# The gate and value stages of a decoder step as straight code, with the index and coefficient tables read in place

## What is computed

```python
q = (xt @ w_query)                     # 8 heads
s1, s2 = q[..., :half] @ k1.T, q[..., half:] @ k2.T
v1, i1 = top_k(s1, 16); v2, i2 = top_k(s2, 16)
top, pos = top_k(v1[:, None] + v2[None, :], 16)
eidx = take(i1 * 128 + i2, pos)        # 8 x 16 = 128 experts a token
g = softmax(top)
hid = einsum("thkd,td->thk", u_tab[eidx], xt)
out = einsum("thk,thkd->td", g * gelu(hid), v_tab[eidx])
```

## Time and profile before

| what | us |
|---|---|
| median of three runs | 1786.53 (1786.04 to 1788.68) |
| the profiled execution | 1785.46 |
| its span, first to last instruction | 1783.8 |
| TensorE busy | 1679.1 |
| VectorE busy | 1403.2 |
| ScalarE busy | 765.6 |
| GpSimd busy | 581.5 |

### The profile page before, as it was taken

One profiled execution on the slowest core, in us unless ns is written; L12 is line 12 of the kernel. 1 busy time (PEld: TensorE's weight loads), 2 busy tenths in 40 slices (PEclk: granted clock), 3 DMA queues, 4 the chain that ended last, 5 costly groups with the idle time before them and its releaser, 6 DMA issues.

```text
span 1783.8 us, 30227 instructions
## 1 busy us (share of the span) xinstructions
PE 1679.1 (94%) x9914; PEld 1487.4 (83%) x9914; DVE 1403.2 (79%) x3186; ACT 765.6 (43%) x1194; POOL 581.5 (33%) x513
## 2 busy tenths in 40 slices
PE   5999998788999999989989999997999999999997
PEld 4999743468999999979989999996888888888885
DVE  3225368446399899969989999997899999999998
ACT  3223145123344432346767777763333333333333
POOL 0000370000445443653333324334333333333331
PEclk9999999799899999999999999998999999999999
DMA  3344451550433332479998999999999999999995
GB/s 117 98 161 149 148 181 42 196 224 1 141 111 131 118 108 96 164 256 357 386 355 311 395 343 382 415 391 371 377 382 386 387 384 383 389 385 383 385 388 184
DMA packets 195266, 470.85 MB, mean 264 GB/s; under 512 B 17971, under 2 KB 100531, under 8 KB 192607
## 3 DMA queue, kind: packets, MB, share of 16 engines
q1 hardware_dynamic: 134430, 254.46, 40.7%
q0 software_dynamic: 50944, 178.96, 26.6%
q10 hardware_dynamic: 9792, 36.18, 5.1%
HBM read 411.97 MB, written 61.32 MB: 265 GB/s over the span
## 4 chain that ended last, share of the span: by engine, by line
PE 40%; DVE 26%; issue 6%; DMA 2%; ACT 1%; DVEq 0%; SPq 0%; ACTq 0%; POOLq 0%
PE va L232 10%; PE va L233 10%; PE va L231 10%; DVE og L1925 3%; DVE gathered L1473 3%; PE hp L231 3%; PE hp L232 3%; PE hp L233 3%; DVE ulo L1949 2%; PE ggp L1869 2%; DVE vw L1473 2%; DVE eq L1732 1%; DVE sc L1684 1%; DVE oh L1924 1%; DVE X L1691 1%
## 5 line engine op out<-in xcount | busy, mean ns | idle before, releaser
L231 PE MATMUL hp<-mid_hi,uhi 128*128 128x384 f32 x1024 | 360.3, 352 | 29.4 <-DVE ulo L1949 18.0
L232 PE MATMUL hp<-mid_lo,uhi 128*128 128x384 f32 x1024 | 349.4, 341 | 0.0
L233 PE MATMUL hp<-mid_hi,ulo 128*128 128x384 f32 x1024 | 347.9, 340 | 0.0
L232 PE MATMUL va<-vlo,ahi 128*128 128x512 f32 x768 | 298.8, 389 | 0.0
L231 PE MATMUL va<-vhi,ahi 128*128 128x512 f32 x768 | 298.8, 389 | 0.0
L233 PE MATMUL va<-vhi,alo 128*128 128x512 f32 x768 | 298.8, 389 | 0.0
L1807 POOL DMA_INDIRECT gathered<-in_v_experts,idx_row x160 | 189.7, 1185 | 331.6 <-DVEq L2252 270.3
L231 PEld LDWEIGHTS hp<-mid_hi,uhi 128*128 128x128 f32 x1024 | 196.2, 192 | 35.1 <-DVE ulo L1949 20.8
L1385 POOL TENSOR_TENSOR ulo<-uw,uhi 128x1024 fp32r<-128x1024 f32 x49 | 123.2, 2515 | 262.0 <-ACT uhi L1381 261.9
L1815 ACT ACTIVATE vhi<-vw 128x1024 fp32r<-128x1024 f32 x128 | 134.8, 1053 | 155.7 <-DMA vw<-in_v_experts 153.4
L232 PEld LDWEIGHTS hp<-mid_lo,uhi 128*128 128x128 f32 x1024 | 196.4, 192 | 0.0
(11 more groups left out here) (337 smaller groups left out, 3355.5 us busy)
## 6 DMA issues: line engine op xcount, KB each, us to landing
uw<-in_u_experts SPq DMA_DIRECT2D x128, 512.0 KB
vw<-in_v_experts SPq DMA_DIRECT2D x128, 512.0 KB
gate_matrix<-gst ACTq DMA_DIRECT2D x12, 2048.0 KB
hidden_values<-gelu_out SPq DMA_DIRECT2D x72, 192.0 KB
hd<-hidden_values SPq DMA_DIRECT2D x16, 768.0 KB
gt<-gate_matrix SPq DMA_DIRECT2D x16, 768.0 KB
uw<-hidden_values SPq DMA_DIRECT2D x16, 768.0 KB
uw<-gate_matrix SPq DMA_DIRECT2D x16, 768.0 KB
```

Source lines behind the costliest of these rows:

```text
L231: nc.tensor.matmul(out, a_hi, b_hi, start=first, stop=False)
L232: nc.tensor.matmul(out, a_hi, b_lo, start=False, stop=False)
L233: return nc.tensor.matmul(out, a_lo, b_hi, start=False, stop=last)
```

## The change

The loops of both stages are unrolled. `over_turns` and the value stage run plain Python loops, so every instruction has a constant address. With that go `idx_row`, `hrow`, `crow`, the copies into them, `keep`, and the semaphores `idx`, `hrow`, `part`, `crow`, `fetched`, `init`, `clear`. Gathers take their index column from `eidx`, dots write to `hid`, and adds read `coef`.

Waits that change: the first u gathers wait for `eidx` itself; `cut` waits for `oh` two chunks back rather than for `part`; a gather of `v` waits for the add that used its buffer (`s0` or `s1`), and in row 0 for the last dot that used it, rather than for all dots; these five are asked for in the order in which their buffers come free, behind the memset of `acc_s`. The order of `ulo`, the last dots and `vlo` on VectorE at the seam stays.

One thing more changes: VectorE's share of expert rows. No row is added with tiles 0 to 3, then 160 x (m - 3)/120 rows are done by tile m, up to tile 123, and none with the last four. VectorE also doesn't wait for the start value of `acc0` ahead of the work on tile 4.

```diff
-        def request(pool, n, pairs=0):
+        def request(pool, n):
             row, b = divmod(n, ROW)
             if n == 0:
+                pool.wait_ge(table_prep, 1)
+            if n == SG:
                 pool.wait_ge(gs["tab"], 1)
-            if n == SG:
-                pool.wait_ge(gs["idx"], LOOK)
-            if row and b == 0:
-                pool.wait_ge(gs["idx"], row + 1 + PAIR_ROWS * pairs)
             if n >= LOOK:
-                pool.wait_ge(gs["dot"], n - LOOK + 1 + PAIR_ROWS * ROW * pairs)
-            fetch(pool, n % LOOK, row % LOOK, b)
+                pool.wait_ge(gs["dot"], n - LOOK + 1)
+            fetch(pool, n % LOOK, row, b)
...
-                dve.wait_ge(table_prep, 2)
-                nc.vector.tensor_copy(idx_row[:, :, 0:SG], eidx[:, 0:LOOK, 0:SG]).then_inc(gs["tab"], 1)
                 dve.wait_ge(table_spread, 16 * SG)
-                nc.vector.tensor_copy(eidx[:, 0:SR, SG:], spread_idx[:]).then_inc(gs["tab"], 1)
-                dve.wait_ge(gs["tab"], 2)
-                nc.vector.tensor_copy(idx_row[:, :, SG:], eidx[:, 0:LOOK, SG:]).then_inc(gs["idx"], LOOK)
+                nc.vector.tensor_copy(eidx[:, :, SG:], spread_idx[:]).then_inc(gs["tab"], 1)
...
-        def fetch_v_row(pool, r, slot, b):
-            if b == 0:
-                pool.wait_ge(xs["idx"], r + 1)
-            pool.wait_ge(xs["fetched"], r * ROW + b + 1)
+        def fetch_v_row(pool, r, b):
+            if r == 0:
+                pool.wait_ge(gs["dot"], users(b, LAST_DOTS)[-1] + 1)
+            elif b < SG:
+                pool.wait_ge(xs["s0"], (r - 1) * SG + b + 2)
+            else:
+                pool.wait_ge(xs["s1"], r + 1)
...
         def over_turns(eng, turn):
-            with eng.Fori(0, NI // 2 - 1) as pair:
-                turn(pair, 0, False)
-                turn(pair, 1, False)
-            turn(NI // 2 - 1, 0, True)
-            turn(NI // 2 - 1, 1, True)
+            for pair in range(NI // 2):
+                for half in range(2):
+                    turn(pair, half, pair == NI // 2 - 1)
...
             def cut(j, u, first=False):
-                pool.wait_ge(gs["part"], 2 * j + u + 1)
                 if not first:
+                    if 2 * j + u >= 2:
+                        pool.wait_ge(gs["oh"], (2 * j + u - 1) * GR)
                     pool.wait_ge(gs["first"], (2 * j + u) * (GR // 2))
...
-            for b in range(ROW):
-                fetch_v_row(pool, 0, 0, b)
+            pool.wait_ge(gs["mm"], NI * N2 + RING)
+            nc.gpsimd.memset(acc_s[:], 0.0).then_inc(xs["s1"], 1)
+            for b in sorted(range(ROW), key=lambda c: users(c, LAST_DOTS)[-1]):
+                fetch_v_row(pool, 0, b)
...
-            def dot(n, out, pair=0):
+            def dot(n):
                 row, b = divmod(n, ROW)
-                dve.wait_ge(gathered[n % LOOK], 16 * (n // LOOK + 1) + 16 * ROW * pair)
-                multiply(dve, n % LOOK, b, out)
-                if b == ROW - 1:
-                    later = row + LOOK + PAIR_ROWS * pair
-                    nc.vector.tensor_copy(idx_row[:, row % LOOK], eidx[:, bass.ds(later, 1)].rearrange("p a b -> p (a b)")).then_inc(gs["idx"], 1)
+                dve.wait_ge(gathered[n % LOOK], 16 * (n // LOOK + 1))
+                multiply(dve, n % LOOK, b, hid[:, row, b:b + 1])
...
                 if e == GX - 4:
-                    dve.wait_ge(gs["dot"], SR * ROW)
-                    nc.vector.tensor_copy(idx_row[:, 0:BR], eidx[:, 0:BR]).then_inc(xs["idx"], BR)
-                    dve.sem_inc(xs["fetched"], ROW)
                     dve.wait_ge(stored[1], 16 * (NI + 1))
...
-                dve.wait_ge(xs["init"], 1)
...
-                over_bodies(dve, body)
+                at = 0
+                for m in range(GT, NK):
+                    c, par = m % GT, m // GT % 2
+                    if c == 0:
+                        dve.wait_ge(gld[par], 32 * (m // (2 * GT) + 1))
+                    weigh(dve, c, par)
+                    rest_of_v(dve, m, c)
+                    while at < min(SR * ROW, SR * ROW * (m - GT + 1) // (NK - 2 * GT)):
+                        add_expert(at)
+                        at += 1
+                    rest_of_a(dve, m, c, par)
```

More of the change, by code:

```diff
@@ L1792, in build @@
         gld = [sem(f"x_gld{i}") for i in range(2)]
[L1793 removed]
+        names = ("a", "ahi", "alo", "vhi", "vlo", "vmm", "s0", "s1", "coef")
         xs = {n: sem("x_" + n) for n in names}
[L1795 removed]
         def load_gates(sp, g, par):
@@ L1889, in turn @@
                 j = 2 * pair + half
+                first = FIRST_DOTS + (pair * PAIR_ROWS + half * ROW) * ROW
                 n = (ROW if last else TURN_ROWS[half]) * ROW
@@ L1897, in turn @@
                     while at < n * (i + 1) // GTI:
-                        ahead = half * ROW * ROW + at + LOOK
-                        if not last or ahead < 2 * ROW * ROW:
-                            request(pool, FIRST_DOTS + ahead, pair)
+                        if first + at + LOOK < TAIL:
+                            request(pool, first + at + LOOK)
                         at += 1
@@ L1963, in turn @@
                     while at < rows_here * ROW * (i + 1) // GTI:
-                        q, b = divmod(at, ROW)
-                        dot(FIRST_DOTS + half * ROW * ROW + at, hrow[:, q, b:b + 1], pair)
+                        dot(first + at)
                         at += 1
-                keep(pair, half, rows_here)
             dve.wait_ge(gs["x2p"], 2)
@@ L2202, in value_on_sync @@
             def value_on_sync(sp):
-                def body(b, first, last):
-                    for q in range(BT // GT):
-                        g = b * (BT // GT) + q
-                        if not (first and q < 2):
-                            sp.wait_ge(xs["alo"], (g - 1) * GT)
-                            load_gates(sp, g, q % 2)
-                        if not (first and q < 2):
-                            for i in range(GT):
-                                sp.wait_ge(xs["vlo"], (g - 1) * GT + i + 1)
-                                sp.dma_start(vw[:, i], A["v_experts"][g * GT + i]).then_inc(vld[i], 16)
                 for i in range(2):
@@ L2216, in value_on_sync @@
                 sp.dma_start(gf[:], A["g_final"].broadcast_to([P, D])).then_inc(ns["ld"], 16)
-                over_bodies(sp, body)
+                for g in range(2, NK // GT):
+                    sp.wait_ge(xs["alo"], (g - 1) * GT)
+                    load_gates(sp, g, g % 2)
+                    for i in range(GT):
+                        sp.wait_ge(xs["vlo"], (g - 1) * GT + i + 1)
+                        sp.dma_start(vw[:, i], A["v_experts"][g * GT + i]).then_inc(vld[i], 16)
             def value_on_scalar(act):
@@ L2280, in value_on_vector @@
-                over_bodies(dve, body)
-            def value_on_gpsimd(pool):
-                pool.wait_ge(gs["mm"], NI * N2 + RING)
-                nc.gpsimd.memset(acc_s[:], 0.0).then_inc(xs["clear"], 1)
-                def body(b, first, last):
-                    at = 0
-                    for i in range(BT):
-                        while at < BR * ROW * (i + 1) // BT:
-                            q, k = divmod(at, ROW)
-                            if not (last and q == BR - 1):
-                                fetch_v_row(pool, b * BR + q + 1, (q + 1) % BR, k)
-                            at += 1
-                over_bodies(pool, body)
```

171 lines of the change are left out of this document (59 added, 112 removed).

## The result

The changed kernel takes 1777.14 us, the median of six runs (1772.75 to 1778.76), against 1786.64 us for the kernel before on the same chip: 0.9946 of its time, 95% interval 0.9932 to 0.996. It is faster by 9.5 us, where 5.7 were forecast. Its profiled execution took 1777.63 us with a span of 1776.1 us, 7.7 us less than the span of 1783.8.

What follows compares the result with a forecast made beforehand. TensorE and the DMA engines were taken as full side by side over gate and value stages. Terms -10.0 - 1.2 - 0.3 - 0.4 + 5.0 + 1.2 = -5.7 us gave 1780.8 us on the median's scale, range 1773.5 to 1790.5.

Steps and rivals of the forecast that it cites:

- The jump: Gate stage: straight turns remove TensorE's 8.1 us stall at the loop's branch back and the slow restart, -10.0 us.
- Turn ends: Gate stage, VectorE: without copy and `keep` the one-hot starts sooner at three turn ends that stall TensorE, -1.2 us.
- the seam: Between gate and value stage: an index-row copy and a wait on VectorE ahead of `ulo` go, -0.4 us.
- Tables: End of the routing stage: two copies less, one on the way to SyncE's next loads, -0.3 us.
- Cadence: Value stage: by tile 119 the new schedule wants 4.7 expert rows more from full DMA engines, +5.0 us.
- The early lead: Value stage start: with no adds ahead of it tile 4 ends sooner, some 5 us of lead, used up by tile 63.
- Fetched code: Value stage: straight code keeps fetching instruction packets through the DMA engines for 390 us more, +1.2 us.
- Rival 2: Value stage: DMA engines have room, so the two last terms vanish: -11.9 us, 1774.6 us; chance 0.26.
- Rival 3: Gate stage: the stall's gain is lost as gathers of the tail land later and VectorE waits: 1786 us; chance 0.15.
- Rival 4: Value stage: fetched code goes through one DMA engine, 15 to 19 us extra, 1795 to 1799 us; chance 0.12.
- The rule on jumps: Value loop: each of five jumps back stalls TensorE, so straight code gives 41 us more, 1740 us; chance 0.01.

Runs made afterwards that it cites:

- e2: The kernel before with only the loop of the gate stage's turns written out, small tables, copies and waits kept: 1779.35 us, ratio 0.9949.
- e9: The changed kernel with expert rows spread evenly from tile 4 to the last and TensorE's value program a loop over 16 tiles again: 1773.45 us, ratio 0.992.
- e10: The changed kernel, its own spread of expert rows kept, with TensorE's value program a loop over 16 tiles again: 1779.21 us, ratio 0.9955.
- e3: The kernel before with only the value stage's six middle bodies written out as straight code, on TensorE too: 1790.01 us, ratio 1.0016.
- e8: The changed kernel with the removed tables allocated again and used by nothing: 1783.24 us, ratio 0.998.
- c_after: The changed kernel, unaltered, run once more beside other kernels on one chip: 1778.88 us, ratio 0.995.
- e7: The changed kernel loading only half of the gate chunks from the third group on, so its output is wrong: 1768.73 us in one run.
- e11: The kernel before with the value stage's six middle bodies straight on all engines but TensorE, which keeps its loop: 1791.54 us, ratio 1.0017.
- e5: The changed kernel with expert rows spread evenly from tile 4 to the very last: 1773.22 us, ratio 0.9917.
- c_even: The changed kernel with expert rows spread evenly from tile 4 to the very last, run a second time: 1775.05 us, ratio 0.9927.

## Why the prediction was right, and where it was not

The sign, the mechanism and the range held: the gain is the jump, and the DMA engines of the value stage take half of it back. The sum was 3.8 us short of the measured 9.5. That it came so near is in part luck: gains of 5 to 6 us were missed or taken too small, and costs were taken some 3 us too small. Term by term:

- **The jump, -10.0: right.** Shown by e2: -10.1 us over the two tiles around it, -9.4 in the gate stage, -8.1 to -9.1 in the runs. Nothing came in its place. There were no more such stalls to remove: e9 and e10, with five jumps back in TensorE's value program, are no slower than their straight twins within the scatter. The section of the Trainium skill that I weighed there ("Runtime: NRT & Kernel Launch", "Instruction fetch mechanics") gives a window of two pages of 16 KiB, and I applied that to TensorE; the same section gives TensorE's instruction memory as 128 KiB, which I passed over. What these traces show agrees with the larger figure: an estimate from the packets of q8, 16 KB each, gives 37 KB for the value stage's looped body (11 packets in 320 us of e3, 65.3 us a body), which was not fetched again, and the gate stage's looped body came in nine and eight packets, some 130 to 150 KB, in each of its two passes.
- **Turn ends, -1.2 with bounds 0 and -1.4, and the seam, -0.4: together too small, as far as one trace of e2 can say.** e8 against e2, both with the old durations, have all of the copies' removal between them: 456.4 to 452.9 us (-3.4 unrounded) in the gate stage, twice the -1.6, with a scatter of up to 3.6 us between traces of the same code. Of the three stalls that the term counted at 1 us or more each, the first was only 0.83 us (at 869.72 us). The stalls behind the ends of the third and the fifth turn explain part: 1.31 us of waiting in e2 at 1004.23 became 0.32 in e8 at 998.00, about 0.8 to 1.0 us each where I took 0.4. I had taken the 0.53 us between copy and one-hot for the whole price of copy, wait for the dots and `keep`; by these two kernels it was more. The first wait of the stage went the other way, `ggp` for `og` 3.6 us in e2, 5.7 in e8 and 6.4 in after. The seam itself shows no gain: from tile 120 to the first `va` 52.9 us before, 52.6 in e8, 51.5 to 54.0 in the other straight kernels. What makes up the rest of the -3.4 is not shown.
- **Tables, -0.3: about right.** From tile 47 to 48 TensorE takes 6.8 us before and 6.3 after, and 6.3 in e8.
- **Missing: the routing stage.** I looked for a cost only in edited lines. The stretch from tile 16 to 32 became 3.6 us faster with no edit in it, by the places of the tiles (e8). In the two traces the gain at tile 48 is only 2.2 us, since tile 16 happened to start 1.7 us later. By the means it is whole: the five traces with the tables start tile 48 at 783.8 us, the nine without at 780.3. e8 and c_after differ by 4.4 us in the medians. This is the largest part of what the sum lacked.
- **Cadence, +5.0 with bounds 0 and +7.5: right in kind, a bit small.** The mean of the four kernels with this cadence is 531.2 us, of the two with the old cadence in straight bodies 525.0: +6.2. The steps hold one by one: TensorE's first loss is at 1515 us, tile 69, where I had the spare time used up "somewhere after tile 60"; there is none in the last four tiles, and e7 shows that DMA time is the cause; the price is 1.1 to 1.3 us a row where 1.27 was taken. The early lead of 5 us is there too: `alo` of tile 4 ends 8.0 us before TensorE comes to that tile, against 2.6 before.
- **Fetched code, +1.2: too small, and its mechanism isn't borne out.** Straight bodies cost 2.7 to 3.2 us (e3, e11), but taking away the fetch of TensorE's code, on which most of the term was built by its packets' share, gives back nothing that the runs show: e11 equals e3, e10 equals after and c_after, e9's ratio lies between those of e5 and c_even. A cost of 1.2 us is below what these runs can tell; what the 3 us are is open.

The rivals. Rival 2, room on the DMA engines, falls: TensorE waited in the value stage in every kernel with this cadence and all of the gate tables, and did not with half of them (e7). Its 1774.6 us is nearer to the measured 1777.1 than my 1780.8, so the time alone would not have told them apart; the trace does. Rival 3, the gain lost in the gathers of the tail, falls: e2 kept it, and VectorE's waits for gathered `u` rows in after are nine and 10.6 us, against eight and 9.7. Rival 4, the fetch through one DMA engine, falls for TensorE's code by e3 and e11: straight bodies cost 3 us and not 15 to 19, with or without it. The rule on jumps falls, for TensorE's value loop, with the earlier trace rows and e9.

The best version is the even cadence, three kernels at 0.9917, 0.9927 and 0.992 of the time before, 3.8 us (c_even against c_after) and 5.8 us (e9 against e10) better than the change side by side. None reaches the 522.0 us of the old value stage together with the shorter gate stage; that would be about 5 us more.

## What to carry to other kernels

Where two resources are full side by side, a gain on one is kept only until the other's next transfer is due, so price every shift of a schedule in bytes: rows ahead of the even rate, times the time that one takes of the full DMA engines, less the lead. Spread such work evenly to the very end, and don't put more pieces of it ahead of an urgent operation than there are buffers. A table that goes out of an allocation moves all that lies behind it, so before a gain is laid to an edit, allocate it again unused. And a term built on a share of packets ("0.3% of the DMA engines") needs its own experiment, one engine's loop put back, before it is believed.

## What the runs showed of the hardware that was not expected

- The same VectorE operation on the same shape took 1591 or 876 ns, another 1283 or 1610 ns, by nothing but the place of its tiles in the on-chip memory; four unused tables turned this back. TensorE's mean pitch per 384-column product in the gate stage moves with it, 174.1 ns in the five traces with the tables, 173.3 to 173.4 in the nine without.
- One jump back in the gate stage cost 10.1 us, 8.15 of them idle and the rest a restart at a clock of 0.65; five jumps back in the value stage cost nothing, on the same engine. In the gate stage the loop's code came over q8 in each pass as straight code does (nine packets from 782 to 932 us, eight from 932 to 1065; 25 from 780 to 1240 us before, 23 in after), in the value stage none came from 1380 to 1700 us.
- TensorE's code, 12 packets of 0.20 MB in 320 us, came through DMA engines that were already full and delayed nothing that could be measured, to within some 2 us.
- The full DMA engines moved 381 to 386 GB/s from 1380 to 1700 us in every kernel that loads all of the bytes, whatever the cadence. The Trainium skill gives about 358 as one core's half of its HBM stack and says that this side binds transfers between HBM and the on-chip memory ("DMA: Bandwidth & Descriptors", "Where 436 GB/s comes from"); this kernel, which uses one core, was above it, in this stage over 320 us.
